# Combining stage with GpSimd weight splits, one contraction for both share parts and work by token chunk; chunk scan over pairs of chunks

## The reference, cut to what matters

```
wts = softmax(stack(lses), axis=0)
o = einsum('gbsh,gbshd->bshd', wts, stack(outs))
y = o * silu(z)          # z = hn @ w_in[:, last 1024 columns]
x = x + y @ w_out
```

## Time and profile before

| | us |
|---|---|
| median of 3 runs | 2709.29 (2705.72 to 2711.34) |
| the profiled execution, its own time | 2707.69 |
| its span in the profile | 2705.5 |
| PE busy | 2404.7 (89% of the span) |
| DVE busy | 1143.0 (42%) |
| ACT busy | 830.7 (31%) |
| POOL busy | 841.3 (31%) |

### The profile page before, as it was taken

The page is one execution under the profiler, slowest core; times in us unless marked ns, Lnnn a source line. Parts: engine busy times, 40 slices in busy tenths (PEclk is TensorE's granted clock), DMA queues, the critical chain, the costliest instruction groups (busy, mean ns, idle before and its releaser), DMA issues. The chain is left out here.

```text
span 2705.5 us, 37956 instructions
## 1 busy us (share of the span) xinstructions
PE 2404.7 (89%) x14002; PEld 1902.1 (70%) x14002; DVE 1143.0 (42%) x2566; ACT 830.7 (31%) x2158; POOL 841.3 (31%) x1291
## 2 busy tenths in 40 slices
PE   5999999999999999999999888869799990458878
PEld 4777777777777777777777576758688770457767
DVE  5243333333333334333333333343323999535434
ACT  4233333333333333333333321122434220133221
POOL 0755555555656655511111101120111110221200
PEclk6999999999999999999999888979899995688989
DMA  4222222222222222221221265455555430674433
GB/s 158 53 64 77 74 93 81 73 73 90 76 74 79 73 82 73 79 84 53 71 61 48 54 225 203 170 191 172 189 167 160 152 96 10 175 214 156 145 134 117
DMA packets 146272, 298.94 MB, mean 110 GB/s; under 512 B 31232, under 2 KB 85504, under 8 KB 142848
## 3 DMA queue, kind: packets, MB, share of 16 engines
q1 hardware_dynamic: 146096, 296.58, 34.7%
HBM read 178.39 MB, written 86.67 MB: 98 GB/s over the span
## 5 line engine op out<-in xcount | busy, mean ns | idle before, releaser
L861 PE MATMUL att_pj<-hT_hi,att_wh 128*128 128x512 f32 (+1 forms) x1728 | 642.7, 372 | 9.8 <-DVE att_wl L715 7.7
L861 PE MATMUL att_pj<-hT_lo,att_wh 128*128 128x512 f32 (+1 forms) x1728 | 613.5, 355 | 0.0
L861 PE MATMUL att_pj<-hT_hi,att_wl 128*128 128x512 f32 (+1 forms) x1728 | 612.7, 355 | 0.0
L728 DVE CUSTOM_DVE_ANT_0 att_pr<-att_sc,att_mask 128x256 f32<-128x256 f32 (+2 forms) x480 | 161.0, 373 | 608.7 <-PE att_sc L804 585.4
L616 POOL TENSOR_TENSOR att_sw<-att_sw,att_rope 128x1280 f32<-128x1280 f32 x48 | 201.2, 4191 | 679.3 <-DMA att_sw<-att_t 679.1
L861 PEld LDWEIGHTS att_pj<-hT_hi,att_wh 128*128 128x128 f32 x1728 | 326.2, 189 | 96.1 <-issue 46.0
L638 ACT ACTIVATE att_pr<-att_pr,att_stats 128x256 f32<-128x256 f32 (+2 forms) x480 | 221.8, 464 | 472.9 <-DVE att_stats L728 472.1
L861 PEld LDWEIGHTS att_pj<-hT_hi,att_wl 128*128 128x128 f32 x1728 | 326.4, 189 | 48.5
L861 PEld LDWEIGHTS att_pj<-hT_lo,att_wh 128*128 128x128 f32 x1728 | 326.8, 189 | 41.3
L672 ACT COPY att_t<-att_pj 128x512 f32<-128x512 f32 (+1 forms) x216 | 111.4, 516 | 486.2 <-PE att_pj L861 486.2
L595 POOL TENSOR_TENSOR att_prod<-att_power,att_ab 128x128 f32<-128x128 f32 x416 | 164.6, 427 | 8.4
(11 more groups left out here) (238 smaller groups left out, 4147.4 us busy)
## 6 DMA issues: line engine op xcount, KB each, us to landing
att_raw<-in_w_att_dram SPq DMA_DIRECT2D x72, 512.0 KB, 3.6
att_sw<-att_t SPq DMA_DIRECT2D x192, 160.0 KB, 2.8
o_scratch<-att_o SPq DMA_DIRECT2D x24, 640.0 KB, 3.5
comb_o<-o_scratch SPq DMA_DIRECT2D x24, 640.0 KB, 6.4
placed_f<-att_place SPq DMA_DIRECT2D x8, 1024.0 KB, 4.5
e_scratch<-att_place SPq DMA_DIRECT2D x8, 1024.0 KB, 4.4
comb_fpre<-placed_f SPq DMA_DIRECT2D x16, 512.0 KB, 4.9
f_scratch<-comb_ft SPq DMA_DIRECT2D x16, 512.0 KB, 3.4
```

Source lines behind the costliest of these rows:

```text
L728: dve.tensor_tensor_reduce(pr[:, n % 2, h, 0:w], sc[:, h, 0:w], mask[:, a:a + w], -SCALE, 3e38, ALU.add, ALU.min, st[:, i, head, 0:1]).the ...
L861: last = pe.matmul(pj[:, c % 3, 0:n], w[:, which, kt], h[:, kt, lo:lo + n], start=(r == 0), stop=(r == CHUNK_MMS - 1))
```

## The change

1. **Combining.** The low parts of the weights are made by POOL, early in its turn of tile n, not by DVE at the end of its own. The two parts of the shares lie in one tile `both`, `ch` on partitions 0 to 47 and `cl` on 64 to 111 (the rest cleared by POOL), and `select` holds its matrix twice, so that one matmul with 128 rows of contraction does what two did. Its DMA grows from 576 KB to 1536 KB. The order is by chunk: behind chunk c of z PE spreads the three groups of chunk c of the tile before; DVE multiplies three, adds two; POOL multiplies the chunk by its gate; SP stores the chunk. The transposes of the shares come at the end of tile 0, and so do ACT's copies of them.
2. **Scan.** `discretize` squares once more, so `dec` holds `A^8` and `A^16` (nine more POOL instructions). The columns of `states` are taken in pairs (163 per row now, the sample starts at 130): after each four groups have left, `carry_over` on DVE adds to each second column what the one before carries into it, then the scan goes from even column to even column in 64 steps, 16 of them with the sample. In the back stage `carry_over` completes the odd columns, 8 groups at a time, one block ahead of the entering copies, from a decay that SP loads first.
3. `raw` of the front stage has one buffer, and its loads run one tile ahead.

```diff
-PARAM_STEPS = 122
+PARAM_STEPS = 131
...
-    for _ in range(3):
+    for squaring in range(4):
...
+        if squaring >= 2:
+            level = dec[:, squaring - 2]
...
@@ combine_stage
-        select = m.sb("select", [GH, UNITS, P], F32R)
-        ch = m.sb("share_hi", [GH, TOK], F32R)
-        cl = m.sb("share_lo", [GH, TOK], F32R)
+        select = m.sb("select", [P, UNITS, P], F32R)
+        both = m.sb("share_parts", [P, TOK], F32R)
+        ch, cl = both[0:GH], both[64:64 + GH]
...
+            def y_store(n):
+                for c, (lo, cnt) in enumerate(CHUNKS):
+                    sp.wait_ge(y_done, NCH * n + c + 1)
+                    sp.dma_start(y_scratch[lo // P:(lo + cnt) // P, :, n].rearrange("i p t -> p i t"),
+                                 y[:, lo:lo + cnt].rearrange("p (i t) -> p i t", t=P)).then_inc(y_stored[c], 16)
...
@@ scalar
+                if n == 0:
+                    act.wait_ge(cleared, 1)
+                    for c, (lo, cnt) in enumerate(CHUNKS):
+                        act.wait_ge(c_turned, c + 1)
+                        act.copy(ch[:, lo:lo + cnt], bc[0:GH, c, 0:cnt]).then_inc(c_hi, 1)
@@ vector
+                for c, (lo, cnt) in enumerate(CHUNKS):
+                    first = NCH * n + c
+                    v = [o[:, n % 2, g, lo:lo + cnt] for g in range(GROUPS)]
+                    for g in range(GROUPS):
+                        dve.wait_ge(spread, GROUPS * first + g + 1)
+                        dve.tensor_tensor(v[g], v[g], bc[:, g, 0:cnt], ALU.mult).then_inc(scaled, 1)
+                    dve.wait_ge(scaled, GROUPS * first + 2)
+                    dve.tensor_tensor(v[0], v[0], v[1], ALU.add).then_inc(added, 1)
+                    dve.wait_ge(scaled, GROUPS * first + 3)
+                    dve.wait_ge(added, 2 * first + 1)
+                    dve.tensor_tensor(v[0], v[0], v[2], ALU.add).then_inc(added, 1)
@@ gpsimd
+            w_split(0)
+            pool.memset(f(both[0:P]), 0.0).then_inc(cleared, 1)
+            w_split(1)
+            for n in range(KT):
                 if n + 2 < KT:
                     w_split(n + 2)
+                for c, (lo, cnt) in enumerate(CHUNKS):
+                    pool.wait_ge(added, 2 * (NCH * n + c + 1))
+                    pool.wait_ge(gated, NCH * n + c + 1)
+                    if n >= 1:
+                        pool.wait_ge(y_stored[c], 16 * n)
+                    pool.tensor_tensor(y[:, lo:lo + cnt], o[:, n % 2, 0, lo:lo + cnt], gate[:, n % 2, lo:lo + cnt],
+                                       ALU.mult).then_inc(y_done, 1)
@@ tensor
+            def spread_shares(n, c):
+                lo, cnt = CHUNKS[c]
+                for g in range(GROUPS):
+                    q = GROUPS * (NCH * n + c) + g
+                    if q < GROUPS:
+                        pe.wait_ge(c_lo, NCH)
                     else:
-                        pe.wait_ge(scaled, q - NCH + 1)
...
+                        pe.wait_ge(scaled, q - GROUPS + 1)
+                    pe.matmul(bc[:, g, 0:cnt], select[:, PAIRS * g + n], both[:, lo:lo + cnt], start=True, stop=True)\
+                      .then_inc(spread, 1)
@@ new function, used in both stages
+def carry_over(dve, done, base, before, after, decay, tmp):
...
+    dve.tensor_tensor(tmp[:, 0], before, own, ALU.mult).then_inc(done, 1)
+    dve.tensor_tensor(tmp[:, 1][:, :, ::-1], before, cross, ALU.mult).then_inc(done, 1)
+    dve.wait_ge(done, base + 1)
+    dve.tensor_tensor(after, after, tmp[:, 0], ALU.add).then_inc(done, 1)
+    dve.wait_ge(done, base + 3)
+    dve.tensor_tensor(after, after, tmp[:, 1], ALU.add).then_inc(done, 1)
@@ ssm_front_stage
-        raw = m.sb("raw", [P, 2, KT, P])
+        raw = m.sb("raw", [P, KT, P])
...
-                if n >= 2:
-                    sp.wait_ge(w_lo, n - 1)
-                sp.dma_start(raw[:, n % 2], w_d[n]).then_inc(raw_in[n % 2], 16)
+                if n >= 1:
+                    sp.wait_ge(w_lo, n)
+                sp.dma_start(raw[:], w_d[n]).then_inc(raw_in, 16)
...
             for n in range(NT):
-                if n + 2 < NT:
-                    w_load(n + 2)
+                if n + 1 < NT:
+                    w_load(n + 1)
...
+            for q in range(HALVES):
+                for g in range(QG * q, QG * q + QG):
...
+                carry_over(dve, paired, 4 * q, st[:, gs, :, 1:SCOLS - 1:2], st[:, gs, :, 2:SCOLS:2], dec[:, 0, gs],
+                           pair_tmp)
...
-                prev = st[:, :, :, bass.ds(c, n, step=PC + 1)]
-                cur = st[:, :, :, bass.ds(c + 1, n, step=PC + 1)]
+                prev = st[:, :, :, bass.ds(2 * c, n, step=SAMPLE_AT)]
+                cur = st[:, :, :, bass.ds(2 * c + 2, n, step=SAMPLE_AT)]
...
-            with dve.Fori(0, SCH // TURN) as q:
+            with dve.Fori(0, SCH // 2 // TURN) as q:
...
-            with dve.Fori(SCH // TURN, PC // TURN) as q:
+            with dve.Fori(SCH // 2 // TURN, PC // 2 // TURN) as q:
@@ ssm_back_stage, gpsimd and vector
+                    pool.wait_ge(whole, 4 * (q // 2 + 1))
...
+                dve.wait_ge(dec_in, 16)
+                complete(0)
                 for q in range(SG // 4):
+                    if q % 2 == 0 and q // 2 + 1 < NB:
+                        complete(q // 2 + 1)
+                    dve.wait_ge(whole, 4 * (q // 2 + 1))
```

More of the change, by code:

```diff
@@ L920, in combine_stage @@
             m.sem(n) for n in ("w_hi", "w_lo", "z_done", "gated", "shares", "exps"))
-        c_turned, c_hi, c_lo, spread, scaled, added, y_done, y_stored = (
-            m.sem(n) for n in ("c_turned", "c_hi", "c_lo", "spread", "scaled", "added", "y_done", "y_stored"))
+        c_turned, c_hi, c_lo, cleared, spread, scaled, added, y_done = (
+            m.sem(n) for n in ("c_turned", "c_hi", "c_lo", "cleared", "spread", "scaled", "added", "y_done"))
+        y_stored = [m.sem(f"y_stored{c}") for c in range(NCH)]
         block = ctx.enter_context(m.block())
@@ L1076, in _ @@
         @block.tensor
         def _(pe):
-            def spread_shares(n, g):
-                for c, (lo, cnt) in enumerate(CHUNKS):
-                    q = NCH * (GROUPS * n + g) + c
-                    if q < NCH:
-                        pe.wait_ge(c_lo, c + 1)
-                    else:
-                        pe.wait_ge(scaled, q - NCH + 1)
-                    w = select[:, PAIRS * g + n]
-                    pe.matmul(bc[:, c, 0:cnt], w, ch[:, lo:lo + cnt], start=True, stop=False)
-                    pe.matmul(bc[:, c, 0:cnt], w, cl[:, lo:lo + cnt], start=False, stop=True).then_inc(spread, 1)
+            def spread_shares(n, c):
[4 more added lines that the diff above has]
+                        pe.wait_ge(c_lo, NCH)
+                    else:
+                        pe.wait_ge(scaled, q - GROUPS + 1)
+                    pe.matmul(bc[:, g, 0:cnt], select[:, PAIRS * g + n], both[:, lo:lo + cnt], start=True, stop=True)\
+                      .then_inc(spread, 1)
@@ L1106, in _ @@
                     last.then_inc(z_done, 1)
-                    if n == 0:
-                        pe.wait_ge(const_in, 64)
-                        pe.wait_ge(shares, SHARES)
-                        for i in range(lo // P, (lo + cnt) // P):
-                            last = pe.transpose(bc[0:GH, c, i * P - lo:(i + 1) * P - lo],
-                                                share[:, i].rearrange("p g h -> p (g h)"), ident[:])
-                        last.then_inc(c_turned, 1)
-                    else:
+                    if n >= 1:
                         if n == 1 and c == 0:
@@ L1119, in _ @@
                         f_turn(2 * n + c)
-            for g in range(GROUPS):
-                spread_shares(KT - 1, g)
+                if n == 0:
+                    pe.wait_ge(shares, SHARES)
+                    for c, (lo, cnt) in enumerate(CHUNKS):
+                        for i in range(lo // P, (lo + cnt) // P):
+                            last = pe.transpose(bc[0:GH, c, i * P - lo:(i + 1) * P - lo],
+                                                share[:, i].rearrange("p g h -> p (g h)"), ident[:])
+                        last.then_inc(c_turned, 1)
+            for c in range(NCH):
+                spread_shares(KT - 1, c)
 def out_stage(nc, name, src, w_d, res, gain, res_out, dest, ident_d, split_w=None, d_stored=None):
@@ L1308 @@
 TAPS = 2 * L - 1
+PAIR_COLS = NC // 2 + 1
+def carry_over(dve, done, base, before, after, decay, tmp):
+    own = decay[:, :, 0].unsqueeze(3).to_broadcast(list(before.shape))
+    cross = decay[:, :, 1, ::-1].unsqueeze(3).to_broadcast(list(before.shape))
+    dve.tensor_tensor(tmp[:, 0], before, own, ALU.mult).then_inc(done, 1)
[4 more added lines that the diff above has]
+    dve.tensor_tensor(after, after, tmp[:, 1], ALU.add).then_inc(done, 1)
 def ssm_front_stage(nc, w_d, h_scratch, skip_d, f_scratch, e_scratch, bb_scratch, c0_scratch, decay_scratch,
@@ L1347, in ssm_front_stage @@
         ps = m.ps("states_ps", [P, 4, 512])
```

(6 more changed lines are left out.)

136 lines of the change are left out of this document (63 added, 73 removed).

## The result

| | before | after |
|---|---|---|
| median of 3 runs, us | 2709.29 (2705.72 to 2711.34) | 2578.65 (2574.60 to 2581.53) |
| ratio to before, 95% interval | | 0.9518 (0.9492 to 0.9544) |
| the profiled execution, its own time | 2707.69 | 2578.65 |
| its span | 2705.5 | 2576.8 |
| PE busy | 2404.7 (89%) | 2375.5 (92%) |

What follows compares the result with a forecast made beforehand. PE was busy nearly everywhere, but 84.6 us of scan ran on DVE alone and transfers bound the back stage. Terms: -50.7 - 84.6 + 10 + 3 + 2 = -120.3 from 2707.7, forecast 2588 us, range 2570 to 2620.

Steps and rivals of the forecast that it cites:

- The step that halved both rows: Scan: half of 83.7 us (32 steps with the sample) and of 147.0 us (96 without), 115.4 us.
- The spreads: Combining: half of the spread matmuls go, 1.74 us per tile, 12.2 us over seven tiles.
- Waits with their clock: Combining: six PE waits for the weights' low part go, 22.0 us, and the half clock behind them, 12.0 us.
- Tile 0: Combining's first tile: PE's 4.1 us wait for the shares goes with 2.0 us of half clock; net gain 1.5 us.
- The back stage: Back stage: decay load and two completions delay the start by 7 us, contention with POOL's copies costs 3: +10 us.
- The single buffer: Front stage: one buffer for raw weights makes loads land barely in time, +3 us (0 to 12).
- Attention: Attention stage: nine more POOL instructions in front of a rotation DVE waits for, +2 us (0 to 3).
- A: Rival: steps of two elements cost 1.96 ns and DVE bounds the back stage, +36 us there, 2614 us; chance 0.17.
- B: Rival: combining becomes bound by transfers or ACT, half of 34 us comes back, 2605 us; chance 0.09.
- C: Rival: in the scan, longer rows of `states` make a step cost twice as much, 2679 us; chance 0.02.
- D: Rival: slower, the single buffer makes PE wait in each front tile, 2715 us; chance 0.02.
- E: Rival: the back stage hides all and PE all the rest, 2573 us; chance 0.10.

Runs made afterwards that it cites:

- order_only: The changed kernel with combining's weight splits back on DVE and each spread matmul issued twice: 2612.03 us, ratio 0.9665, combining 203.9 us.
- back_act: The changed kernel with POOL's entering copies in the back stage made by ACT: 2576.21 us, ratio 0.9519, back stage 99.7 us.
- scan_alone: The changed kernel with `combine_stage` and `select` as before the change: 2634.88 us, ratio 0.9738.
- dve_split: The changed kernel with combining's weight splits back on DVE, all else kept: 2602.27 us, ratio 0.9624, combining 193.8 us.

## Why the prediction was right

- **The bottleneck was read rightly.** The scan's tail was the only thing in 84.6 us, and PE bounds what is left (307.9 of 327 us busy). The last scan step ends at 2167.7, 12 us before the last front matmul. Front and gap gave 77.6 us; the sum had 81.6.
- **But the scan took 127.7 us, not 115.4.** The step that halved both rows is wrong. It takes every part of the scan's time as shrinking with the count, and a step as dear as before. Timelines of POOL and of DVE, kernel after:

```profile
2044.15 2.40 POOL L1498 TENSOR_TENSOR front_wl<-front_raw,front_wh 128x1024 fp32r<-128x1024 f32 x1 [16.64 <-ACT front_wh L1459]
...
2067.51 2.43 POOL L1498 TENSOR_TENSOR front_wl<-front_raw,front_wh 128x1024 fp32r<-128x1024 f32 x1 [8.53 <-ACT front_wh L1459]
```

```profile
2044.18 2.84 DVE L1551 TENSOR_TENSOR states<-states,front_pair_tmp 128x256 f32 x1
2067.66 2.68 DVE L1547 TENSOR_TENSOR front_pair_tmp<-states,front_decay 128x256 f32<-128x256 f32 x1
```

  While POOL makes the low part of a weight, one scan instruction of 0.4 to 0.6 us takes 2.2 to 2.8 us. Six splits fell beside the scan before, and six do after. The six steps that meet one are longer than the ordinary step by 12.2 us in sum before and by 12.4 after; I had halved that part, which is 6.3 of the missing 12.3 us. Most of the rest is in the ordinary steps themselves. Timelines of DVE from the last instruction of one step to the first of the next, before and then after:

```profile
2301.73 0.40 DVE L1513 TENSOR_TENSOR states<-states,front_t 128x128 f32 x1
2302.16 0.39 DVE L1508 TENSOR_TENSOR front_t<-states,front_decay 128x128 f32<-128x128 f32 x1
...
2160.99 0.40 DVE L1551 TENSOR_TENSOR states<-states,front_pair_tmp 128x128 f32 x1
2161.53 0.40 DVE L1546 TENSOR_TENSOR front_pair_tmp<-states,front_decay 128x128 f32<-128x128 f32 x1
```

  The instructions last as long as before, but this last one is followed after 0.54 us and not 0.43. A single step takes 1.58 us and not 1.47, a double one 2.48 and not 2.34, which makes some 7 us over 48 and 16 steps. The step's addresses are now worked out from `2 * c`; whether that is the cause was not tried. POOL's 16 short adds for the kernels are not it: after the change the steps that meet no split add nothing to the ordinary length in sum, where before they added 2.5 us, whose half is saved too. The scan also began 9.0 us later in its stage than before (183.0 against 174.0), where the sum had 6.1. It was slack and no merit of the sum that nothing came of this: of the 25 us forecast between the scan's end and the stage's, 12.9 were left up to SP's last store of the stage (2180.65). What had been said of the room for the `carry_over`s was misread too, on the safe side: of DVE's 189 us before, 141 were scan and not 77, and ahead of the scan it was busy 48 of 177 us.
- **Combining gave 55.7 us, not 50.7.** Against the terms: the six steady tiles 52.3 (six times 8.71) where the six waits, their half clock and six tiles' spreads made 44.4; the first two tiles -1.4 where I had +1.5 and 1.7 of spreads; the tail 4.8 where I had 3. The spreads were sized rightly (1.74 us a tile; 19.03 - 17.32 = 1.71). Waits with their clock were undersized: 5.67 us a tile forecast, 26.03 - 19.03 = 7.0 measured. I had read the half clock from one stretch of 4.0 us at 0.50 behind one wait; a whole tile at 0.87 shows more of it (3.1 us of PE's time, 22.2 against 19.1). And the move to GpSimd was not all of it: by itself it is worth 4.21 us a tile (21.53 - 17.32). What order_only keeps of the change gives 2.95: its waits are 2.70 us and not 3.67, and PE's own time falls by 2.0 us in the mean, with less of the lower clock (four of its six tiles have 0.93 and two 1.00, where before has four with 0.87 and two with 0.93). That last adds over one chunk, and not over 1280 tokens, shorten the wait fits this, but the order was not tried apart from the 128-row spreads and the share copies. The term had credited GpSimd with all of it.
- **Tile 0 gave nothing.** The wait of 4.1 us for the shares did not go. It stands as one of 4.8 us for `share_parts` (3.7 to 4.8 in eight traces, where the old code has 3.9 to 4.6), since PE still needs both parts before it can spread. The first wait became 12.1 from 11.0, as the 1.3 us for POOL's split said. The stage's first two tiles are 1.4 us longer in this pair of traces, but that is scatter: the eight traces with the new combining end them 49.6 to 51.7 us after the stage's start, the three with the old one at 50.0 to 51.1. The term of 1.5 us, and 1.7 of spreads, did not come.
- **The back stage** was right in sum (+7.8, forecast +10) and in its main term: the load of block 2 goes out 7.1 us later, against 7. The contention is there (back_act), but the 3 us for it are not shown: without it the stage is 1.3 us shorter, within the scatter, and its blocks still wait for their loads. With traces of equal code 7.7 us apart in this stage, the sum's closeness is in part luck.
- **The single buffer** cost no wait of PE for a weight. The front's matmuls end 4.1 us later in the mean of the traces, near the 3 forecast, and with late inputs for the kernels, which the prediction had named behind the split; but that the buffer is the cause is not shown.
- **Attention** gave 3.0 us where I had forecast 2 lost. The step itself was right: SP's first store of `att_o` goes out at 167.1 to 167.7 us in the three traces with the old parameter steps and at 168.9 to 171.2 in the eleven with the nine more, +2.4 in the mean, and from there every unit takes the same time in all. What the forecast did not know is a clock that differs from run to run at the stage's end (1.00 or 0.50 in the eleven traces with this code, last section); it gave this trace about 5.5 us, which is luck.
- **The rivals.** A (1.96 ns for steps of two elements) fell with 1.16 in the back stage and 1.28 in the front. B fell: the DMA share rose to 0.78 in the stage and 0.89 in a tile, more than the 0.74 forecast, and one wait of 0.3 us for a transfer came of it. C fell, since 64 steps took 127.7 us where twice the old price would have kept the 230 of before. D fell. E (2573) is 6 us below the result, the forecast 9 us above; but E is not what happened, since the back stage lost 7.8 us and did not hide all. By stage the forecast was high by 5 us in attention, 5 in combining and 2 in the back stage, and low by 4 in front and gap, which took part of that back.

## What to carry to other kernels

Undo each part alone and both together before a gain is credited to one: here the work by chunk and what came with it were worth 2.95 us a tile beside the 4.21 of the move that was meant. When a loop is halved, split its time first into what shrinks with the count and what comes from other engines' instructions beside it, which did not shrink here (12.2 us before, 12.4 after), and read the length of one new step from the trace before calling it as long as the old. And when work is moved ahead of a stage, follow its inputs through the DMA queue too: a small load behind two blocks' loads left the stage 2.5 us longer. Where traces of the same code differ by 5 to 8 us in a stage, take several before reading a gain of 3.

## What the runs showed that I had not expected

**The last unit of attention runs at one of two clocks.** Busy time of 1520 to 1530 and 1530 to 1540 us: after,

```profile
1520.00:1530.00 10.00, 8.40 (x73) 6.21 (x71) 3.34 (x20) 5.70 (x25) 0.00 (x0) 1.00 0.17 67
1530.00:1540.00 10.00, 8.89 (x74) 5.12 (x76) 6.67 (x31) 7.75 (x32) 0.00 (x0) 1.00 0.00 0
```

and scan_alone, with the same code in this stage.

```profile
1520.00:1530.00 10.00, 8.55 (x70) 6.21 (x68) 3.32 (x19) 5.67 (x25) 0.00 (x0) 0.93 0.16 66
1530.00:1540.00 10.00, 10.00 (x50) 5.32 (x50) 4.70 (x25) 5.86 (x23) 0.00 (x0) 0.50 0.01 2
```

Both start the unit at the same place (first store at 169.75, units of 63.1 and then 58.0 us). PE then has only attention's own matmuls, no projection beside them, with short pauses, and the second execution is granted half the clock for them: 50 matmuls and not 74 in ten microseconds. The stage ends at 1545.4 in the one and at 1551.0 in the other. Of the eleven traces with this code five show 1.00 from 1530 to 1540 us (ends of 1544.9 to 1545.7) and six 0.50 (1550.6 to 1553.2); the three with the old code all show 0.50 or 0.51 there (1548.4 to 1549.5). So attention's 5 us of the 9 by which the forecast was high are of this kind. Differences of 5 us between single traces mean little here unless the stage is named.

**A short DVE instruction beside a POOL subtraction took about as long as that.** In the front stage DVE's instruction of 0.4 to 0.6 us that meets a GpSimd subtraction takes 2.2 to 2.8 us, while POOL's has 2.4 to 2.6 (up to 2.8 before the change). In the back stage DVE's copies of 1024 elements take 1151 ns beside POOL and 691 without, and before the change it was the short ones that paid: 1127 ns for 256 elements, where back_act has 288. What makes DVE wait the lengths do not show. I had cited a doubling in the prediction and not seen that a short instruction can pay more: four to six times its length in the scan.

**A wait of 2.94 us has two prices.** In dve_split four tiles that have it show a clock of 0.92 and two 1.00, and they differ by 1.6 us. With the waits of 2.70 us in order_only it is 0.93 in four and 1.00 in two. With the 3.67 us of before all six are below 1.00: 0.87 in four and 0.93 in two.
